# Layer one of the first mixture's experts: all passes over one half of the weights before the other half

## What is computed, cut to what matters

```python
top_v, top_e = lax.top_k(logits, TOP_K)                 # TOP_K = 4, N_EXPERTS = 32
def expert_block(args):
    tok, e = args
    hcat = x_pad[tok] @ w1[e] + b1[e]                   # 1024 -> 2048, "layer one"
    x_glu = jnp.minimum(hcat[:, ::2], SWIGLU_LIMIT)
    x_lin = jnp.clip(hcat[:, 1::2], -SWIGLU_LIMIT, SWIGLU_LIMIT)
    act = x_glu * jax.nn.sigmoid(SWIGLU_ALPHA * x_glu) * (x_lin + 1.0)
    return act @ w2[e] + b2[e]                          # 1024 -> 1024, "layer two"
```

## Time and profile before

| | us |
|---|---|
| median of 3 runs (2395.27 to 2398.16) | 2396.15 |
| the profiled execution, its own time | 2396.02 |
| its span, first to last instruction | 2394.2 |
| around the span | 1.8 |
| stage of the first mixture, first bias matmul of expert 0 to the last matmul of layer two of expert 31 | 443.0 to 1508.2 |
| TensorE busy over the span | 1884.6 (79%) |
| VectorE, ScalarE busy over the span | 811.5, 496.6 |

### The profile page before, as it was taken

One profiled execution on the slowest core, in us unless ns is written; L12 is line 12 of the kernel. 1 busy time (PEld: TensorE's weight loads), 2 busy tenths in 40 slices (PEclk: granted clock), 3 DMA queues, 4 the chain that ended last, 5 costly groups with the idle time before them and its releaser, 6 DMA issues. The chain is left out here.

```text
span 2394.2 us, 28273 instructions
## 1 busy us (share of the span) xinstructions
PE 1884.6 (79%) x11518; PEld 859.9 (36%) x11518; DVE 811.5 (34%) x1618; ACT 496.6 (21%) x1005; POOL 76.6 (3%) x96
## 2 busy tenths in 40 slices
PE   6999998888889887788887887679967755555565
PEld 3655545433333333333333323245534422222221
DVE  2224332333332343433343333586395200000001
ACT  2022201222232133332233323212200210000000
POOL 0000000000000000000000000192000000000000
PEclk9999998899999999899988998799988887877877
DMA  7745258388888699998999989332214579999996
GB/s 274 262 142 187 76 195 305 148 353 364 328 367 337 265 394 398 422 424 331 368 424 423 416 361 418 110 138 71 74 37 153 214 307 428 428 428 422 428 428 273
DMA packets 113954, 713.53 MB, mean 298 GB/s; under 512 B 16703, under 2 KB 21006, under 8 KB 68654
## 3 DMA queue, kind: packets, MB, share of 16 engines
q1 hardware_dynamic: 105344, 704.98, 72.5%
q10 hardware_dynamic: 8398, 5.47, 0.8%
HBM read 709.35 MB, written 1.07 MB: 297 GB/s over the span
## 5 line engine op out<-in xcount | busy, mean ns | idle before, releaser
L434 PE MATMUL ps<-ar 128*128 128x128 f32 (+5 forms) x1750 | 385.8, 380 | 115.6 <-PEq L692 84.9
L780 PE MATMUL ps<-ring,ar 128*32 128x512 f32 x3072 | 357.2, 611 | 23.5 <-DMA ring<-in_w 22.4
L441 PE MATMUL ps<-ring,ar 128*32 128x512 f32 x1536 | 209.4, 706 | 193.0 <-DMA ring<-in_w_up 80.8
L434 PEld LDWEIGHTS ps<-ar 128*128 128x128 f32 (+2 forms) x1750 | 248.5, 208 | 248.7 <-issue 211.9
L434 PE MATMUL ps<-ring,ar 128*128 128x512 f32 (+2 forms) x624 | 263.1, 582 | 8.5 <-DVE ar L1237 3.1
L1538 DVE TENSOR_TENSOR ar<-ps,ar 128x512 f32<-128x512 f32 x180 | 124.5, 692 | 284.4 <-PE ps L434 282.0
L780 PEld LDWEIGHTS ps<-ring,ar 128*32 128x32 f32 x3072 | 95.9, 112 | 282.0 <-issue 247.3
L790 PE MATMUL ps<-ring,ar 128*32 128x512 f32 x1536 | 174.7, 595 | 21.6 <-ACT ar L2179 21.6
L538 PE MATMUL ps<-ring,ar 128*128 128x512 f32 x384 | 172.9, 598 | 15.6 <-ACT ring L2242 15.6
L441 PEld LDWEIGHTS ps<-ring,ar 128*32 128x32 f32 x1536 | 59.8, 127 | 336.6 <-issue 335.7
L434 PEld LDWEIGHTS ps<-ring,ar 128*128 128x128 f32 x624 | 119.2, 193 | 147.0 <-issue 135.4
(11 more groups left out here) (387 smaller groups left out, 1312.2 us busy)
## 6 DMA issues: line engine op xcount, KB each, us to landing
ring<-in_w SPq DMA_DIRECT2D x192, 2048.0 KB, 16.7
ring<-in_w_gate SPq DMA_DIRECT2D x32, 2048.0 KB, 18.4
ring<-in_w_up SPq DMA_DIRECT2D x32, 2048.0 KB, 16.7
ring<-in_w_down SPq DMA_DIRECT2D x32, 2048.0 KB, 16.7
ring<-in_w_in SPq DMA_DIRECT2D x21, 2048.0 KB, 8.1
ring<-in_w_ada SPq DMA_DIRECT2D x12, 2048.0 KB, 8.7
ring<-in_w_out SPq DMA_DIRECT2D x4, 2048.0 KB, 7.8
ring<-in_w_branch SPq DMA_DIRECT2D x6, 1024.0 KB, 5.0
```

The lines of the kernel that those rows point to most:

```text
L434: ins = self.t.e.matmul(o, l, r, start=(i == 0), stop=(i == len(pairs) - 1))
L441: ins = self.t.e.matmul(b[32 * i:32 * i + 32, :], l, r, start=(k == 0), stop=(k == len(steps) - 1))
L780: ins = e.matmul(b[32 * s:32 * s + 32, :], l, r, start=(k == 0), stop=(k == 8))
```

## The change

Layer one is cut into halves of the weights: half 0 is the bias and the chunks 0 and 1, half 1 the chunks 2 and 3. All four banks are claimed ahead of the first matmul. For each half, pass 0 runs over it, then the further passes over the same half, in one `either` whose body holds the `If`s for the passes 2 and 3 nested in one another; then the two slots of that half are freed. `pe["l1", u, 0]` is the end of pass 0 in the second half. The numbers of matmuls, their shapes and the order of the transfers are the same.

```diff
-            def layer1(b, n, arrive):
-                W = []
-                steps = [[(pick, B1R[:, HALF(s)]) for s in range(4)]]
-                for c in range(4):
-                    W.append(RG_(slot["w1", u, c], 0, 2, 2048))
-                    steps += [[(HG[:, 2 * c + r, 32 * n:32 * n + 32], W[c][:, r, HALF(s)]) for s in range(4)]
-                              for r in range(2)]
-                for k, four in enumerate(steps):
-                    if arrive and k % 2:
-                        w.weights("w1", u, k // 2)
-                    for s, (l, r) in enumerate(four):
-                        ins = e.matmul(b[32 * s:32 * s + 32, :], l, r, start=(k == 0), stop=(k == 8))
+            def layer1(b, n, half, arrive):
+
+                if half == 0:
+                    for s in range(4):
+                        e.matmul(b[32 * s:32 * s + 32, :], pick, B1R[:, HALF(s)], start=True, stop=False)
+                for c in (2 * half, 2 * half + 1):
+                    if arrive:
+                        w.weights("w1", u, c)
+                    W = RG_(slot["w1", u, c], 0, 2, 2048)
+                    for r in range(2):
+                        for s in range(4):
+                            ins = e.matmul(b[32 * s:32 * s + 32, :], HG[:, 2 * c + r, 32 * n:32 * n + 32],
+                                           W[:, r, HALF(s)], start=False, stop=(c == 3 and r == 1))
                 return ins
...
-            pe["l1", u, 0] = t(layer1(w.claim("l1", u, 0, lane=(0,)), 0, True))
-
-            b = [w.claim("l1", u, n, lane=(n,)) for n in (1, 2, 3)]
+            bl = [w.claim("l1", u, n, lane=(n,)) for n in range(4)]
             count = e.value_load(flag(u))
-            for n in (3, 2):
-                with e.If(count > 32 * n):
-                    layer1(b[n - 1], n, False)
-            either(t, u, 32, lambda: t(layer1(b[0], 1, False)), count)
-            pe["l1x", u] = t.n
-            for c in range(4):
-                w.free("w1", u, c)
+            for half in range(2):
+                done = t(layer1(bl[0], 0, half, True))
+
+                def further():
+                    with e.If(count > 64):
+                        with e.If(count > 96):
+                            layer1(bl[3], 3, half, False)
+                        layer1(bl[2], 2, half, False)
+                    t(layer1(bl[1], 1, half, False))
+
+                either(t, u, 32, further, count)
+                for c in (2 * half, 2 * half + 1):
+                    w.free("w1", u, c)
+            pe["l1", u, 0], pe["l1x", u] = done, t.n
```

## The result

The changed kernel takes 2516.5 us (median of 4 runs, 2513.2 to 2518.9) against 2395.7 us before (2392.6 to 2398.2): ratio 1.0504, 95% interval 1.0486 to 1.0522. The forecast was 2506 us in 2452 to 2556. The profiled execution took 2513.16 us, with a span of 2511.4 us.

A forecast was written before the change was run, and what follows sets the result against it. The prediction took PE's chain with its gaps, not the weights, to bound the stage. Its terms, 176 + 60 - 49 - 42 - 28, gave +117 us; it took +110 on 2396.0 us, so 2506 us, range 2452 to 2556.

The forecast's parts named there:

- Part 1: Claims of banks 1 to 3 ahead of pass 0: PE waits for ScalarE's evictions of layer two, +176 us.
- Part 2: Start of layer one: slow clock behind the longer idle times, 2.3 us at each of 26 places, +60 us.
- Part 4: `spread` gets its full clock back, 2.35 us at each of 18 places, -42 us.
- Part 3: Skips of further passes: old gaps of 104 us go, new else branches and some fetching come, net -49 us.
- Part 5: Weights in layer one: waits for late weights and 6 us of slow passes go, -28 us.
- A: Rival, larger loss: skips keep their price under a saturated DMA, clock down in both halves; +165, 2561 us; chance 0.12.
- B: Rival, smaller loss: instruction waits vanish, half a pass hides the fetch; about +60, 2456 us; chance 0.18.
- D: Rival, no difference: the wait fills only time in which PE waits for weights anyway; 2396 us; chance 0.02.
- C: Rival, faster: evictions between layer two and the next layer one don't hold PE; -60, 2336 us; chance 0.05.

The follow-up runs named there:

- e1: Kernel before with one edit: banks 1, 2 and 3 claimed ahead of pass 0, whole passes and freeing as before; 2531.9 us, ratio 1.0568.
- e2: Changed kernel with banks 1 to 3 claimed inside the condition's body in half 0, only where further passes exist; 2357.5 us, ratio 0.9839; run again 2353.5 us.
- e8: Changed kernel with the claims of banks 1 to 3 moved behind pass 0's first half, unconditional; 2383.0 us, ratio 0.9942.
- e9: Changed kernel with 6 whole-array matmuls added per expert between the claim of bank 0 and those of banks 1 to 3; 2493.3 us, ratio 1.04.
- e3: Kernel before with its further passes in one nested condition, one branch over 432 instructions instead of three over 144; 2392.8 us, ratio 0.998.
- e4: Changed kernel with three separate conditions per half, over 64 or 80 instructions each, instead of one nested condition; 2516.3 us, ratio 1.0498.
- e6b: Repeat of e6, all four slots freed together, on the same chip as the repeat of e2: 2364.8 us against 2353.5 us.
- e6: e2 with all four slots of w1 freed together behind the second half instead of by halves; 2361.0 us, ratio 0.9852.
- e7: Kernel before, whole passes, with further passes in one nested condition and banks 1 to 3 claimed inside its body; 2389.5 us, ratio 0.9969.
- e5: Changed kernel with 24 more bias matmuls per expert between the claim of bank 0 and those of banks 1 to 3; 2573.8 us, ratio 1.0749.

## Why the prediction was right, and which terms weren't

The sign, the cause and the time were right: 2506 forecast, 2516.5 measured. That the sum came so near is in part luck: I had parts 1, 2 and 4 too low by 17, 15 and 10 us and part 3 too high by 44, and the errors cancel. Term by term, from the views above and the same groups of the kernel before:

| part | forecast | measured | from |
|---|---|---|---|
| 1, claims ahead of pass 0 | +176 | +193 | idle ahead of the bias 213.0, before 20.3 |
| 2, slow starts of layer one | +60, -6 in part 5 | +69 | 480.3 against 411.1 busy |
| 3, skips and instruction waits | -49 | -93 | 104 before, 10.7 after |
| 4, `spread` | -42 | -32 | 128x512 records of L434: 175.2, then 143.0 |
| 5, late weights | -22 | -22 | 22.4 to nothing |
| sum | +117 (+110 taken) | +115 | stage +121.5, span +117.2 |

The 20.3 us are the waits ahead of the bias for VectorE (10.1 + 1.4), ACT (0.7) and L692 (8.1); the 10.7 are 4.9 + 4.7 and 1.1 for VectorE. The remaining 6 us of the stage I did not place.

**Part 1** was right in mechanism, shown by e1, e2 and e8, and 17 us short. The last eviction ends 7.68 us behind layer two as I read, but the bias starts only 0.5 us behind that (0.49 to 0.60 at 30 of the 31 places, once 0.74); I had 0.1. e1 shows what makes most of it. It waits for the same four banks and starts its bias 0.14 or 0.15 us behind the last eviction at all 31 places. What stands between the claims and the first matmul in the changed kernel and not in e1 is the register load `e.value_load(flag(u))`: some 0.37 us each time, 11 us in all (211.7 against 200.5). No run moves the load by itself.

**Part 2** was right in mechanism (e9), and the net of two misses in size. By the timeline the records of the first bias and first half take 7.6, 7.5 and 6.9 us in the mean behind one, two and three passes, against 4.7 at full clock: 86 us over 31 places, where I had 60 over 26. Part of this is a choice that failed: I gave nothing to the 2.7 us behind three passes, as nearer to an idle 2.01 that slowed nothing. Behind an idle 3.08 us the first half took 1.55 + 4.79 us (the timeline at 560.57): slow too. Against it, some 17 us of the old slow passes went, where I had 6.

**Part 3** is the term that was wrong in size, and beyond my bounds (-64 to 0). I had charged each new else branch 0.95 us, from the gap behind layer two. But that gap holds two else branches and a wait for VectorE; the new ones cost 0.15 to 0.19 us. And next to nothing was left of the fetching (two waits of 0.9 and 1.6 us). The rule of the Trainium skill, page "Runtime: NRT & Kernel Launch", section "Instruction fetch mechanics" (two blocks of 256 instructions, a stall on a taken branch out of them), pointed the right way: by it some 35 us more would come back, and 44 did. Part of the traces agrees with it: 84.9 us for three skips of 144 in a row, 73.0 for one of 432 (e3), 4.9 and 4.7 us for 240 and 192 with half a pass between them, and 3.4 and 4.0 in e4. Part does not follow from the length alone: 40.0 us for the same three skips in e1, and waits of 2.0 to 2.3 us at a skip of 192 in e8. How full the DMA is goes with it each time.

**Part 4** came out at -32. I had 2.35 us of slow clock at each of 18 places, 42 us in all, but the 296 records of `spread` took only 38 us more than 37 times 3.70, and 6 of these are still there. **Part 5**: the late weights went, DMA share 0.82 as forecast; the slots that come free sooner gave nothing in this kernel, as said, and 4 to 11 us in e2 (e6b), where the weights bound again.

**The rivals.** A, the larger loss, is out for this kernel: the 84.9 us went to 4.9. What it supposed, that skips cost more under a full DMA, is what e2 and e8 look like. B, the smaller loss, had its instruction waits right, yet the time wrong, because parts 1 and 2 were not smaller. D is out, since the waits were ten times what PE had spent on late weights. C named the right place from the other side: take the evictions out of the way and it is faster, which is e2 at 2357 us, where I had 2336. Its 480 us at a DMA share of 1.00 are 240 in the rows and some 420 in the whole trace.

## What to carry to other kernels

A claim of a buffer is a wait in the engine's stream; when loops are cut or interleaved, the claims must not travel with the allocation to the top, but stay behind the work that covers their last reader, or inside the condition that needs them. Before moving one, read from the trace when the last reader ends against when the claim is reached: here 7.7, 4.8 or 2.6 us against 0.95 or less, at 31 places. What else stands between a claim and the first instruction behind it is paid too: here a register load, 0.37 us each time. And a skip over a long body gets cheaper if it is cut in two with work between: the cut passes gave some 28 us here (e6 against e7), and the waits at the skips stay larger where the weights fill the DMA.

## What the runs showed that I had not expected

The granted clock fell to 0.50 while PE was busy, with matmuls of 32 rows on 32x32 weights (e5: 48 records in 8.9 us at 511.98, and the layer one behind them slow), and stayed at 1.00 in the same place with 12 records of the whole array (e9). So a PE that the profile calls busy doesn't have its clock kept by that alone. Nor does the length of an idle time settle it: nothing is slow behind the idle 2.01 us of rows 4, and in e9 the pass behind an idle 2.06 us is. The Trainium skill, page "TensorE: Matmul & The Clock Gate", Part 1, describes a clock that is low by default and released by activity; e9's filler agrees with it, and e5 shows that a PE which the profile calls busy may still not hold it.
